# Two transformer blocks of 256 tokens on one core: wide value units, one product for two halves of the input, and heads put in another order

## The reference

```python
# first block, layer i (0: differential attention, 1: neighbourhood attention)
sh1, sc1, g1, sh2, sc2, g2 = split(silu(c) @ ada_w[i] + ada_b[i], 6)   # modulation, the context has its own
h = rmsnorm(x, norm_mix[i]) * (1 + sc1) + sh1
q, k, v = split(h @ wqkv, 3)                 # context tokens too
x = x + g1 * (attention(q, k, v) @ wo)
h2 = rmsnorm(x, norm_ffn[i]) * (1 + sc2) + sh2
x = x + g2 * conv_ffn(h2, up, conv, conv_b, down)
# second block, hybrid layer l (after the first block's closing rmsnorm)
proj = rmsnorm(x, norm_g[l]) @ w_in[l]
o = (nsa(...), pool(...), conv(...), fox(...))     # fox: logf = log_sigmoid(f_logit + bias), c = cumsum(logf)
for n in range(4):
    branch = (o[n] * silu(gates[:, :, n])) @ w_branch[n]
    acc += sigmoid(merge[:, :, n]) * branch
x = x + acc @ w_out                          # a last rmsnorm follows the second layer
```

## Time and profile before

| | us |
|---|---|
| median of 3 runs (lowest to highest) | 1661.72 (1661.22 to 1662.11) |
| the profiled execution's own time | 1660.64 |
| its span in the trace | 1658.5 |
| PE busy | 1606.6 (97%) |
| PE's weight loads | 1404.6 (85%) |
| DVE busy | 890.6 (54%) |
| ACT busy | 749.2 (45%) |
| POOL busy | 545.7 (33%) |
| mean granted clock of TensorE | 0.987 of full |
| DMA | 249.39 MB, mean 150 GB/s |

### The profile page before, as it was taken

How to read it: one execution, slowest core, us unless ns; L and a number is a source line. 1 busy time by engine, 2 the same in 40 slices (tenths; PEclk the granted TensorE clock), 3 DMA queues, 4 the chain that set the end, 5 groups by cost and what they waited for, 6 DMA issues and landing times.

```text
span 1658.5 us, 26678 instructions
## 1 busy us (share of the span) xinstructions
PE 1606.6 (97%) x10956; PEld 1404.6 (85%) x10956; DVE 890.6 (54%) x1406; ACT 749.2 (45%) x1359; POOL 545.7 (33%) x358
## 2 busy tenths in 40 slices
PE   7999988999999999999999999998999999999998
PEld 4779557778767888778968999998999999899998
DVE  4334584455524554342265888548575457668434
ACT  5223584444313443243375655445544444554443
POOL 2214253322202222121172111024423577423554
PEclk9999999999999999999999999999999999999999
DMA  9264601443255222357224454554435545533551
GB/s 395 82 254 156 229 1 52 153 155 143 86 187 187 94 78 79 136 203 230 99 54 155 148 184 155 175 174 147 161 123 174 179 149 172 178 128 127 178 195 60
DMA packets 52984, 249.39 MB, mean 150 GB/s; under 512 B 20608, under 2 KB 21760, under 8 KB 26368
## 3 DMA queue, kind: packets, MB, share of 16 engines
q1 hardware_dynamic: 44400, 244.42, 42.4%
q10 hardware_dynamic: 8464, 3.28, 1.0%
HBM read 246.63 MB, written 1.05 MB: 149 GB/s over the span
## 4 chain that ended last, share of the span: by engine, by line
PE 86%; DVE 6%; ACT 3%; issue 1%; DMA 1%; POOL 1%; ACTq 1%; SPq 0%; POOLq 0%; DVEq 0%
PE psq L528 17%; PE psq L529 17%; PE psq L530 17%; PE ps L528 6%; PE ps L529 6%; PE ps L530 6%; PE ps L541 2%; PE psq L883 2%; PE psq L884 1%; PE psq L885 1%; DVE WL L510 1%; PE ps L1304 1%; PE psq L2122 1%; PE ps L1293 1%; PE psq L1261 1%
## 5 line engine op out<-in xcount | busy, mean ns | idle before, releaser
L528 PE MATMUL psq<-NH,WH 128*128 128x256 f32 (+1 forms) x1640 | 519.8, 317 | 3.9 <-DVE NL L793 2.0
L510 DVE TENSOR_TENSOR WL<-RAW,WH 128x1024 fp32r<-128x1024 f32 (+3 forms) x264 | 320.2, 1237 | 368.4 <-ACT WH L500 368.2
L529 PE MATMUL psq<-NL,WH 128*128 128x256 f32 (+1 forms) x1640 | 513.4, 313 | 0.0
L530 PE MATMUL psq<-NH,WL 128*128 128x256 f32 (+1 forms) x1640 | 513.3, 313 | 0.0
L510 POOL TENSOR_TENSOR WL<-RAW,WH 128x1024 fp32r<-128x1024 f32 (+2 forms) x116 | 302.3, 2608 | 556.2 <-ACT WH L500 543.8
L500 ACT ACTIVATE WH<-RAW 128x1024 fp32r<-128x1024 f32 (+2 forms) x380 | 361.0, 1000 | 177.7 <-DMA RAW<-wstream 127.2
L528 PEld LDWEIGHTS psq<-NH,WH 128*128 128x128 f32 x1640 | 314.2, 192 | 33.4 <-issue 12.0
L530 PEld LDWEIGHTS psq<-NH,WL 128*128 128x128 f32 x1640 | 314.1, 192 | 18.1
L529 PEld LDWEIGHTS psq<-NL,WH 128*128 128x128 f32 x1640 | 314.3, 192 | 16.8
L528 PE MATMUL ps<-NH,WH 128*128 128x256 f32 (+1 forms) x376 | 124.6, 331 | 0.0
L529 PE MATMUL ps<-NL,WH 128*128 128x256 f32 (+1 forms) x376 | 123.5, 328 | 0.0
(11 more groups left out here) (349 smaller groups left out, 2845.8 us busy)
## 6 DMA issues: line engine op xcount, KB each, us to landing
RAW<-wstream SPq DMA_DIRECT2D x196, 1024.0 KB, 4.9
RAW<-wstream SPq DMA_DIRECT2D x32, 704.0 KB, 4.1
K<-first SPq DMA_DIRECT2D x4, 1024.0 KB, 16.7
X<-xin SPq DMA_DIRECT2D x2, 1024.0 KB, 6.2
V<-first SPq DMA_DIRECT2D x2, 1024.0 KB, 19.2
Q<-first SPq DMA_DIRECT2D x2, 1024.0 KB, 24.9
BR<-rpb ACTq DMA_DIRECT2D x8, 256.0 KB, 10.0
BR<-rpb SPq DMA_DIRECT2D x8, 256.0 KB, 8.5
```

The source lines that it names most:

```text
L510: e.tensor_tensor(WL[:, u % 3, a:z], RAW[:, v % 3, a:z], WH[:, u % 3, a:z].bitcast(F32), ALU.subtract).then_inc(w_lo_p if pool else w_lo_v, 1)
L528: e.matmul(o, lh, rh, start=start, stop=False)
L529: e.matmul(o, lh, rl, start=False, stop=False)
L530: return e.matmul(o, ll, rh, start=False, stop=stop)
```

## The change

1. **Value units.** Units 8 to 11 of both layers hold 4 k blocks of 512 columns in place of 8 of 256. Two units make one half of the values: the products of `pe_values` run into four banks, one for each token tile, 12 for each tile and unit, 512 columns wide. ACT reads a bank of 512 columns at once when the second unit of a pair is through.
2. **Both halves at once.** High and low parts of the activations lie side by side (NHL, HHL). For 256 tokens `mm_both` makes one product of 512 columns (WH with high and low part) and one of 256 (WL with the high part) in place of three of 256. It is used for units 0 to 2 of wo and for down in layer 1 of the first block, for the merge units of the last three branches and for units 0 to 2 of w_out in the second. The banks' two halves are added on reading: DVE in two steps for residuals; for merges ACT copies the second half (`act_merge_half`), DVE adds the first (`dve_merges`), and ACT takes Tanh in SBUF (`act_merge_tanh`). The merge units use the bank pairs 2, 7 and 0, 1 in turn.
3. **Turns of the attention's outputs** come at the end of their step, behind the scores.
4. **Modulation row 5** is made in two parts of four units with 1024 parameters: row 5 within layer 1's q and k units, as before its first four; row 6 around the sums after wo and ahead of the first two up units. ACT's and DVE's split of the weights of up unit 1 (two ahead of wo unit 3) comes behind the norm's instructions (`act_finish`, `dve_finish`).
5. **Heads of the hybrid layers.** On ACT the copy of QF, the copies for the compression and a weight split come ahead of Abs, Exp, Ln and Tanh; on DVE a low part of the weights comes ahead of the first rotation (`dve_turn`). The turns of LF and what follows from them (`act_decay`, `dve_decay`) lie between the two compression units.

In all PE issues 8201 rows in place of 9287.

```diff
-QKV_ADA = {("qkv", 1, 4): (0, 1, 2, 3), ("qkv", 1, 6): (4,), ("qkv", 1, 7): (5,), ("qkv", 1, 0): (6,), ("qkv", 1, 1): (7,)}
+QKV_ADA = {("qkv", 1, 4): (0, 1, 2, 3)}
+LATE_ADA = {("up", 1, 0): (0, 1, 2), ("up", 1, 1): (3,)}
 ...
+            for k in range(ada_units(5)):
+                add_ada(5, k)
 ...
+        for k in {0: (0, 1, 2), 1: (3,)}.get(j, ()):
+            add_ada(6, k)
 ...
+    if kind == "qkv" and key[2] >= 8:
+        return 4, 512
 ...
+        NHL = sb("NHL", [P, 2, DT, 512], F32R)
+        NH, NL = NHL[:, 0, :, :], NHL[:, 1, :, :]
 ...
+                c = k if b < 5 else 2 * k + j // 2
+                mm = e.matmul(AB[32 * j:32 * j + 32, :], CB[:, c, :], RAW[:, v % 3, 512 * j:512 * j + 512],
+                              start=k == 0, stop=k == ada_units(b) - 1)
 ...
+        def mm_both(e, o, wh, wl, x, start, stop):
+            e.matmul(o[:, 0:512], wh, x, start=start, stop=False, skip_group_check=True)
+            return e.matmul(o[:, 0:256], wl, x[:, 0, :], start=False, stop=stop, skip_group_check=True)
 ...
+                    mm = mm_both(e, outs[j], wh[:, k, w], wl[:, k, w], NHL[:, :, k, 0:256], k == 0, k == DT - 1)
 ...
+        def pe_values(e, l, i):
+            key, pr, kh = ("qkv", l, 8 + i), i // 2, i % 2
+            v, wh, wl = weights(key)
+            for t in range(4):
+                if i == 3:
+                    (pe_na_qk if l else pe_diff_qk)(e, t)
+                if i == 0 and t % 2 == 0:
+                    e.wait_ge(qk_sb, qk_outputs_before(l, 7 + t // 2))
+                if i == 2 and t == 3:
+                    e.wait_ge(ada_par, 5 if l else 1)
+                c = slice(t * P, t * P + P)
+                for k in range(4):
+                    if t == 0:
+                        wait_weights(e, v, k)
+                    kk = 4 * kh + k
+                    mm = mm3(e, bank[4 * pr + t], NH[:, kk, c], NL[:, kk, c], wh[:, k, :], wl[:, k, :], kk == 0, kk == 7)
+                if kh or t == 3:
+                    mm.then_inc(gemm, 1)
         def act_qkv(e, l):
 ...
+                for t in range(4 if i % 2 else 0):
+                    if i == 3 and t < 2:
+                        (act_na_exp if l else act_diff_exp)(e, t)
+                    e.wait_ge(gemm, product(key, t))
+                    e.activation(V[l][:, t, 256 * (i - 1):256 * (i - 1) + 512], bank[4 * (i // 2) + t],
                                  ACT.Copy).then_inc(v_sb, 1)
                 if l == 1 and i == 2:
                     e.activation(STAT[:, 11, 16:17], ONE, ACT.Exp)
 ...
-                    if age == 11 and qt == 3 and h < 7:
-                        pe_out_turn(e, h)
 ...
+                j = n - 11
+                if 0 <= j < 28 and diff_job(j)[1] == 3:
+                    pe_out_turn(e, j // 4)
+                if n == 2:
+                    e.wait_ge(v_sb, 8)
 ...
+                        pe_both(e, ("wo", 1, 1), bank[2:4], (0, 1), range(6), wait_x)
+                        pe_both(e, ("wo", 1, 0), bank[0:2], (0, 1), (6, 7), wait_x).then_inc(gemm, 1)
 ...
+            pe_ada(e, 6 if l else 3, 0)
             pe_sums(e, n, 6)
             if l == 0:
                 pe_ada(e, 3, 1)
             pe_sums(e, n, 7)
             if l == 0:
                 pe_ada(e, 3, 2)
+            else:
+                pe_ada(e, 6, 1)
 ...
+                if (l, i) != (1, 3):
+                    split_hi(e, ahead(("wo", l, i)))
 ...
+        def dve_residual_both(e, p, m, o):
+            x, gain = X[:, m, 0:256], ada_param(1, p, m, 0)
+            e.scalar_tensor_tensor(out=x, in0=o[:, 256:512], scalar=gain, in1=x, op0=ALU.mult,
+                                   op1=ALU.add).then_inc(x_low, 1)
+            e.wait_ge(x_low, m + 1 if p == 2 else 7 + m)
+            e.scalar_tensor_tensor(out=x, in0=o[:, 0:256], scalar=gain, in1=x, op0=ALU.mult,
+                                   op1=ALU.add).then_inc(x_res, 1)
 ...
+                    if l == 1 and j < 2:
+                        pe_ada(e, 6, 2 + j)
+                    if l == 1 and j == 6:
+                        pe_ada_turn(e, 6)
 ...
+                        if l:
+                            mm = mm_both(e, down_bank(m), wh[:, k, :], wl[:, k, :], HHL[:, :, kk, :], kk == 0,
+                                         kk == nj - 1)
 ...
+            for name in ("vn", "qf", "kf", "vf"):
                 pe_proj(e, l, name)
-            e.wait_ge(fx_v, FXV * l + 7)
-            for q in range(2):
-                mm = e.transpose(bank[3][:, q * P:q * P + P], LF[:, q, :], IDENT)
 ...
+            act_plain(e, l, "qf", QF[:, :, :], 0.125)
+            for kind in range(2):
+                if kind == 0:
+                    e.wait_ge(flat, 5 * l + 5)
+                f = FLT[:, kind, :].rearrange("p (k n) -> p k n", k=16)
+                e.activation(FHV[:, kind, :, 0, :], f, ACT.Copy).then_inc(flat_hi, 1)
 ...
-            act_plain(e, l, "kf", KF[:, :, :])
+            act_out_of(e, l, "kf", KF[:, :, :])
+            act_plain(e, l, "vf", VF[:, :, :])
 ...
+            lo_prep(e, l, "qf", False)
             dve_turn(e, l, 0, QN[:, :, :])
 ...
+                if kind == 0:
+                    e.wait_ge(fx_v, FXV * l + 7)
+                    for q in range(2):
+                        mm = e.transpose(bank[3][:, q * P:q * P + P], LF[:, q, :], IDENT)
+                    mm.then_inc(fx_tr, 1)
 ...
+                    act_decay(e, l)
 ...
+                    dve_decay(e, l)
 ...
+            return (bank[2], bank[7]) if (q % 2 == 0) == (q < 4) else (bank[0], bank[1])
 ...
+                e.wait_ge(m_sum, 24 * l + 2 * before[-1] + 2)
 ...
+            q = 4 * (n - 1) + j
+            merge_free(e, l, q)
+            v, wh, wl = weights(unit_key(l, f"m{n}{j}"))
+            for c, o in enumerate(merge_banks(q)):
+                for k in range(DT):
+                    if c == 0:
+                        wait_weights(e, v, k)
+                    w = slice(P * c, P * c + P)
+                    mm = mm_both(e, o, wh[:, k, w], wl[:, k, w], NHL[:, :, k, 0:256], k == 0, k == DT - 1)
+                mm.then_inc(gemm, 1)
 ...
+        def act_merge_half(e, l, n, j, c):
+            q = 4 * (n - 1) + j
+            e.wait_ge(gemm, product(unit_key(l, f"m{n}{j}"), c))
+            e.activation(M[:, n % 2, 2 * j + c, :], merge_banks(q)[c][:, 256:512], ACT.Copy).then_inc(m_half, 1)
+        def act_merge_tanh(e, l, n, j):
+            q, t = 4 * (n - 1) + j, M[:, n % 2, 2 * j:2 * j + 2, :]
+            e.wait_ge(m_sum, 24 * l + 2 * q + 2)
+            e.activation(t, t, ACT.Tanh, scale=0.5).then_inc(m_tanh, 1)
+        def act_merges(e, l, n):
+            for j in range(4):
+                split_hi(e, ahead(unit_key(l, f"m{n}{j}")))
+                if n >= 2:
+                    e.wait_ge(br_v, 16 * l + 4 * (n - 2) + j + 1)
+                act_merge_half(e, l, n, j, 0)
+                if j:
+                    act_merge_tanh(e, l, n, j - 1)
+                act_merge_half(e, l, n, j, 1)
+            act_merge_tanh(e, l, n, 3)
+        def dve_merges(e, l, n):
 ...
+                lo_merge(e, l, n, j, False)
+                for c in range(2):
+                    t = M[:, n % 2, 2 * j + c, :]
+                    e.wait_ge(m_half, 24 * l + 2 * q + c + 1)
+                    e.tensor_tensor(t, merge_banks(q)[c][:, 0:256], t, ALU.add).then_inc(m_sum, 1)
 ...
+                    pe_both(e, ("out", l, i), outs, (0, 1), range(DT), wait_x if i == 0 else nothing).then_inc(gemm, 1)
 ...
+                e.scalar_tensor_tensor(out=x, in0=o[:, :, 256:512], scalar=0.5, in1=x, op0=ALU.mult,
+                                       op1=ALU.add).then_inc(x_low, 1)
+                e.wait_ge(x_low, 14 + 3 * l + i + 1)
+                e.scalar_tensor_tensor(out=x, in0=o[:, :, 0:256], scalar=0.5, in1=x, op0=ALU.mult,
                                        op1=ALU.add).then_inc(x_res, 1)
 ...
+            split_hi(e, ahead(("wo", 1, 3)))
```

242 lines of the change are left out of this document (135 added, 107 removed).

## The result

The changed kernel takes 1645.80 us in the median of 4 runs (1642.10 to 1647.73), the kernel before 1661.47 in the runs beside it. The ratio is 0.9908 with an interval of 0.9884 to 0.9932: faster by 15.7 us, 0.9%, where 38 were forecast.

What follows compares the result with a forecast made beforehand. PE's own time and its waits were taken to bound the kernel. Terms of −12.0, −16, −4, −7.9 and +1.5 summed to −38.4 us, from 1661.72 to a median of 1623, range 1613 to 1641.

Steps and rivals of the forecast that it cites:

- Heads: Hybrid layers' heads: PE's waits before vf go and the clock stays full; −16 us, poor end −5.
- The first rival: The clock falls all the same in the heads and at up's start, giving back 8 to 9 us: 1631; chance 0.2.
- Products: PE's matrix products: fewer, wider ones save time in values and in groups of three; −12.0 us, poor end −4.2.
- value products: Value units: 768 products of 256 columns become 384 of 512 at 227 ns each; −4.8 us.
- joined products: 528 groups in wo, merges and w_out gain 12.6 ns each, −6.7 us; down's 176 groups add −0.5.
- Down: FFN down products: 176 groups, 352 ns before and 352 or 347 after; −0.5 us, between 0 and −0.9.
- The second rival: The wide products save nothing, leaving −26.4 us and a median of 1635; chance 0.12.
- Turns: Attention outputs: six waits before moved turns are covered by PE work; −4 us, ends −1.5 and −6.4.
- Modulation units and the split: Moved modulation units fill waits, the bias-load wait goes, the norm starts earlier, up's clock holds; −7.9 us, ends −3 and −8.5.
- New costs: Two-step residuals, later values and second attention's start, merge hand-over at nothing; +1.5 us, ends 0 and +4.
- the rival on the slower side: Merges' bank hand-over by ACT and DVE stalls PE over 24 units; with 2 us each, 1671; chance 0.03.

Runs made afterwards that it cites:

- experiment 1: Changed kernel with DVE scaling X before Q's rotation and making the first compression unit's low part before K's rotation; 1635.92 us, 0.9845 of the kernel before.
- experiment 5: Changed kernel with ACT emptying the banks of layer 0's last q and k unit before its weight split, not after; 1640.51 us.
- experiment 10: Changed kernel with ACT's and DVE's split of up unit 1 back ahead of the last residuals of wo in layer 1; 1653.47 us.

## Why the prediction was right or wrong

**What bounds the kernel** was read rightly: PE's own time and its waits.

**Heads, −16 forecast, −4.4 in the profiles and 3.0 in the medians: the step that failed.** "The wait goes whole" was true of vf (the 4.8 and 3.6 us are not in the list after and came back with the old order). "Without the wait PE's stream has no gap and I expect the full clock" was not. I had asked what else was late for LF and found cover, and had not asked it for the other things that the compression units wait for. The scaling of X stood on DVE behind K's rotation, its end came 1.5 us after PE was there, and in the changed kernel's profile 7.9 us went by the clock behind that idle time. The first rival had the fall of the clock and its size (8 to 9 us), but as something that would stay, and not as bound to a wait that the change itself uncovers. The runs show that most of the sum was there to be had: with two DVE steps moved (experiment 1), the reordering brings 12.9 us by the medians and, from the kernel before, 14.9 by the stages.

**Products, −12.0 forecast.** The value products run at 227 ns as forecast: layer 1 gains 2.6 us with its last unit, the half of the forecast's 4.8 and a little. In layer 0 that gain was overdrawn by a wait that I had not seen, +2.8, of which some 1.7 are a draw of the clock (experiment 5). The banks of the last q and k unit are needed one unit earlier than before, and ACT stood at a split (experiment 5). For the joined products the term was mis-sized: a group takes 353 ns in merges, in wo and in the second layer's w_out, 6 below three narrow ones, where 346.8 had been added up from the pitches of pure streams (227 and 120). Down takes 7.72 us for a column of 22 groups where it took 7.83, both from the first product to the sums behind the last:

```profile
1062.14:1069.86 7.72, 7.72 (x47) 1.00 0.50 179
```

that is 5 ns a group, −0.9, at the good end of the forecast. For merges, w_out and wo it is 1.9 + 1.7 + 0.2 = 3.8 against 6.7. The second rival (nothing is saved) was wrong: undoing the join costs 5.0 us, 7.1 ns for each of the 704 groups. The Trainium skill, "TensorE: Matmul & The Clock Gate", section "Back-to-back issue gap", has 2.5 ns as the fixed part of the spacing of a product at full clock, and gives it for an isolated product. By that page it would be 1.8 us in all, an estimate; the runs show more, and they decide.

**Turns, −4 forecast, −0.9 by the experiment and −1.6 for the whole stage.** That is at the range's poor end or below it. What was named as unbounded, the loop over the exponential, is what PE now waits for.

**Modulation units and the split, −7.9 forecast.** The q and k stage of layer 1 came out 6.4 below without its value units' 1.9, where −5.3 (four units and the wait behind the bias loads) were forecast; the rest lies in smaller waits. From the last wo products to the first up product it is +0.9 with three units in it, in place of +3.0 with nothing hidden. The first up products take 6.49 where they took 7.99, at the full clock that was forecast, with 0.2 of waiting and a little more than the 5.8 of a pure stream. So this term was right within about two us, but with luck. In the changed kernel's profile the clock stayed up behind the wait of 1.8 us before the sums; in 10 of the 11 experiments with that wait alone it fell there, and the stage took 28.5 to 30.5 us, 2 to 4 above the 26.5 of the kernel before. That DVE's and ACT's split stands behind the norm I had priced at 1.4 (half of 2.54 us is 1.27); in the new load order, putting it back costs 7.7 (experiment 10), and what deferring it brings in the old order was not tested.

**New costs, +1.5.** In the merges nothing waits for the hand-over of the banks, so the rival on the slower side was rightly thought unlikely; there is no row for it in the list of waits.

The sum missed because four parts fell short the same way: the first layer's head, layer 0's banks, the joined products and the turns. The first two are waits that the change uncovered, of 1.5 and 2.4 us, which cost 9.7 and 4.3 in the changed kernel's profile.

## What to carry to other kernels

When a wait goes, list everything that the next instructions wait for, and put the finish time of each beside PE's new arrival; the second latest takes the place of the first, and a step that has not moved can be it. A short wait is not priced by its length alone: 1.5 us cost up to 10 here, and where it can't be removed, even useless products in it can pay. Look at a place in more than one profile before you call its clock good or bad. And take the price of a mixed group of products from a measured mixture, not from pure streams.
